# Chunked scan of an RWKV-7 layer: products paired on the array's quadrants, level operands in three buffers

## The reference, cut to what matters

```python
def rwkv_scan(r, decay, k, v, a_vec, b_vec, s0):
    def step(s, inp):
        r_t, w_t, k_t, v_t, a_t, b_t = inp
        sa = jnp.einsum('bhij,bhj->bhi', s, a_t)
        s = s * w_t[:, :, None, :] + sa[..., None] * b_t[:, :, None, :] + v_t[..., None] * k_t[:, :, None, :]
        return s, jnp.einsum('bhij,bhj->bhi', s, r_t)
    s, o = lax.scan(step, s0.astype(jnp.float32), xs)
```

## Time and profile before

| | us |
|---|---|
| three runs | 3109.29, 3109.90, 3113.63 (median 3109.90) |
| profiled execution | 3110.74 |
| its span | 3109.1 |
| mean granted TensorE clock of it | 0.974 |
| TensorE busy | 2955.9 (95%) |
| VectorE, ScalarE, GpSimd busy | 1796.6, 1132.4, 793.0 |
| the scan, first product to end | 1099.9 to 1329.5 |

### The profile page before, as it was taken

One profiled execution on the slowest core, in us unless ns is written; L12 is line 12 of the kernel. 1 busy time (PEld: TensorE's weight loads), 2 busy tenths in 40 slices (PEclk: granted clock), 3 DMA queues, 4 the chain that ended last, 5 costly groups with the idle time before them and its releaser, 6 DMA issues. The chain is left out here.

```text
span 3109.1 us, 65634 instructions
## 1 busy us (share of the span) xinstructions
PE 2955.9 (95%) x27498; PEld 2794.9 (90%) x27498; DVE 1796.6 (58%) x2864; ACT 1132.4 (36%) x2182; POOL 793.0 (26%) x884
## 2 busy tenths in 40 slices
PE   8999999998999989979899989999998999999998
PEld 8999999998999978838777569999998999999998
DVE  7777774565545656566554552343325877775445
ACT  5333334343112233344664351221143433334333
POOL 3555451023001124240003000000015455553003
PEclk9999999998999999979999999999998999999999
DMA  6566568554422120011015641212123466667763
GB/s 174 177 196 202 184 194 246 173 176 135 129 73 65 55 90 4 18 28 48 11 46 171 220 170 51 52 41 65 31 78 100 138 193 194 190 195 228 220 184 111
DMA packets 416735, 393.37 MB, mean 127 GB/s; under 512 B 50584, under 2 KB 367809, under 8 KB 415674
## 3 DMA queue, kind: packets, MB, share of 16 engines
q1 hardware_dynamic: 383418, 277.05, 29.8%
q0 software_dynamic: 31984, 112.13, 11.0%
q10 hardware_dynamic: 1040, 0.00, 0.0%
HBM read 283.59 MB, written 105.53 MB: 125 GB/s over the span
## 5 line engine op out<-in xcount | busy, mean ns | idle before, releaser
L2167 PE MATMUL banks<-hid_pieces,dn_high 128*128 128x258 f32 x2464 | 452.9, 287 | 7.5 <-DVE hid_pieces L2109 7.5
L1911 PE MATMUL banks<-x_pieces,gate_pieces 128*128 128x258 f32 x3360 | 415.2, 283 | 1.0 <-DVE sq L2005 0.9
L1911 PE MATMUL banks<-x_pieces,up_pieces 128*128 128x258 f32 x3360 | 414.4, 283 | 0.0
L1911 PEld LDWEIGHTS banks<-x_pieces,gate_pieces 128*128 128x128 f32 x3360 | 408.9, 189 | 1.7 <-DVE sq L2005 1.4
L1911 PEld LDWEIGHTS banks<-x_pieces,up_pieces 128*128 128x128 f32 x3360 | 408.6, 189 | 0.2 <-ACT sq L1947 0.2
L2167 PEld LDWEIGHTS banks<-hid_pieces,dn_high 128*128 128x128 f32 x2464 | 386.1, 192 | 8.1 <-issue 7.9
L2167 PE MATMUL banks<-hid_pieces,dn_part 128*128 128x258 f32 x1232 | 349.5, 284 | 0.0
L1167 PEld LDWEIGHTS banks<-XG,pR 128*128 128x128 f32 (+1 forms) x1800 | 286.1, 189 | 10.4 <-issue 6.1
L1167 PE MATMUL banks<-XG,pR 128*128 128x344 f32 (+1 forms) x1800 | 291.5, 323 | 3.7 <-DVE pR L2702 2.9
L1167 PE MATMUL banks<-XR,mg_gate 128*128 128x344 f32 x1728 | 283.3, 319 | 1.3 <-PEq L53 1.3
L1167 PEld LDWEIGHTS banks<-XR,mg_gate 128*128 128x128 f32 x1728 | 273.9, 188 | 1.6 <-issue 1.6
(11 more groups left out here) (567 smaller groups left out, 5499.0 us busy)
## 6 DMA issues: line engine op xcount, KB each, us to landing
hid_spill<-h_stage SPq DMA_DIRECT2D x44, 516.0 KB, 4.2
chain_slot<-hid_spill POOLq DMA_DIRECT2D x64, 258.0 KB, 3.8
t_sums<-chain_slot POOLq DMA_DIRECT2D x64, 258.0 KB, 2.7
dn_low<-w_sums SPq DMA_DIRECT2D x32, 384.0 KB, 3.6
praw<-in_w_in SPq DMA_DIRECT2D x24, 512.0 KB, 4.2
sq<-in_w_in SPq DMA_DIRECT2D x24, 512.0 KB, 4.1
chain_slot<-in_ffn_down POOLq DMA_DIRECT2D x46, 256.0 KB, 4.2
w_sums<-chain_slot POOLq DMA_DIRECT2D x46, 256.0 KB, 3.3
```

The source lines that it names most:

```text
L1911: ins = k.nc.tensor.matmul(out, self.w[m][:, a, w, f * P:(f + 1) * P], self.x[p][:, b, x, f * TQ:(f + 1) * TQ], start=first and f == 0 and ...
L2167: ins = k.nc.tensor.matmul(k.ps[2 * j + q][:, 0:TQ], a[s][:, f * P:(f + 1) * P], k.hid_pieces[m % 2][:, q, f, b, :], start=m in self.FRESH ...
```

## The change

It rewrites the scan's order on four engines; the arithmetic stays.

- Outputs move between halves. `inner`, the first half of `outer`, `solved`, the values' part of the carry and the new transposed inverse write to the other half (q' = 1 - q), the second half of `outer` stays on q' = q, and the two are issued alternately, head by head. The outputs of the even chunk alternate with `inner` in level 8, reading the state alternates with the values' part of the odd carry in level 4 and with the odd state's update in level 16.
- The transposed inverse of level 0 is made by TensorE from Tm (`turned_inverse`, 16 products a round) and copied by ScalarE; VectorE's two operations for it go. The transposed sums of both chunks lie in one bank (3) and are added by one operation of 512 columns (`TTs`).
- ScalarE copies G1 and G2 raw; GpSimd masks the parts that outputs and carries read (`G1r`, `G2`). Tm of both chunks is masked and gets its identity in one operation each.
- Level operands lie in a ring of three buffers (`masked`), so a mask waits for the product three before it.
- g1 and g3 of the next round are issued in level 32; the even chunk's carry too. After the loop the last two chunks are finished one after the other.
- `SampleStep` uses two banks instead of three for its transposes.

```diff
-    Tm, NT_, Ym, Wm, Um = (two((4 + 2 * m) * NU) for m in range(5))
+    TTs = [work[:, 2 * z * NU:2 * (z + 1) * NU] for z in R2]
+    Tm, Ym, Wm, Um = (two(m * NU) for m in (4, 8, 10, 12))
+    both_Tm = work[:, 4 * NU:6 * NU].rearrange("p (s h c) -> p s h c", s=2, h=RT)
+    ring = [view(work, m * NU, CH) for m in (6, 7, 15)]
-    Yb, Zb, Wb, Sb, Ob = (0, 1), (2, 3), 5, 6, 7
+    Yb, Zb, TTb, Wb, Sb, Ob, pair, grams = (0, 1), (2, 4), 3, 5, 5, 7, (6, 7), (5, 6)
...
+    def masked(s, i):
+        return ring[(2 * i + s) % 3]
...
+                        n = 2 * (len(LV) * p + i) + s
+                        if n >= 3:
+                            m = (n - 3) // 2
+                            pe_s.wait(pool, ("Y", m // len(LV), (n - 3) % 2, LV[m % len(LV)]))
...
+            def turned_inverse(p):
+                dve_s.wait(pe, ("TmI", p))
+                if p:
+                    dve_s.wait(pe, ("TT", p - 1, LV[-1]))
+                for s in R2:
+                    ins = both(lambda h, q: mm(lane(half(TTb, s * NU, CH), h, 1 - q), lane(Tm[s], h, q),
+                                               k.ident[64 * q:64 * q + 64, 64 * q:64 * q + 64]))
+                pe_s.done(ins, ("TTi", p))
...
-                pe_s.done(both(lambda h, q: mm(lane(half(Yb[s], 0, CH), h, q), lane(NT_[s], h, q), lane(Tm[s], h, q))),
-                          ("Y", p, s, l))
+            def inner(p, s, l, h):
+                for q in R2:
+                    ins = mm(lane(half(Yb[s], 0, CH), h, 1 - q), lane(masked(s, len(LV) * p + LV.index(l)), h, q), lane(Tm[s], h, q))
+                return ins
...
+            def outer_turned(p, s, h):
+                for q in R2:
+                    ins = mm(lane(half(TTb, s * NU, CH), h, q), lane(Ym[s], h, q), lane(TT[p % 2][s], h, q))
+                return ins
+
+            def outer(p, s, h):
+                for q in R2:
+                    ins = mm(lane(half(Zb[s], 0, CH), h, 1 - q), lane(TT[p % 2][s], h, q), lane(Ym[s], h, q))
+                return ins
...
                 for l in LV:
+                    for s in R2:
+                        inner_open(p, s, l)
+                        for h in H4:
+                            ins = inner(p, s, l, h)
+                            if past and l == 8:
+                                last = output(a, 2 * s + h // 2, h % 2)
+                        pe_s.done(ins, ("Y", p, s, l))
...
+                    if l == 32 and more:
+                        gram(p + 1, "g1")
+                        gram(p + 1, "g3")
...
+                    for s in R2:
+                        outer_open(p, s, l)
+                        for h in H4:
+                            ins = outer_turned(p, s, h)
+                            if l < LV[-1]:
+                                ins = outer(p, s, h)
+                        pe_s.done(ins, ("Z", p, s, l))
...
+                    if l == 32:
+                        carry_even(2 * p)
+                        if more:
+                            turned_inverse(p + 1)
...
                     for s in R2:
-                        dve_s.done(nc.vector.tensor_tensor(G1[z][s], half(s, 0, 2 * CH), k.gram_mask, ALU.mult), ("G1", p, s))
...
+                    dve_s.done(nc.vector.tensor_tensor(TTs[z], TTs[z], k.ps[TTb], ALU.add), ("TT", p, l))
```

More of the change, by code:

```diff
@@ new lines, in turned_inverse, with carried_state @@
+            def turned_inverse(p):
+                dve_s.wait(pe, ("TmI", p))
+                if p:
+                    dve_s.wait(pe, ("TT", p - 1, LV[-1]))
[3 more added lines that the diff above has]
+                pe_s.done(ins, ("TTi", p))
+            def carried_state(c, first):
+                kn, out = now(k.A, 0, c), half(Wb, 0, CH)
+                return both(lambda h, q: mm(lane(out, h, 1 - side(c, q)), lane(kn, h, q), lane(ST[c % 3], h, q),
+                                            start=first and h == 0, stop=not first and h == RT - 1))
@@ L440, in carried_state, with carried_value, carry_even @@
+            def carried_value(c, h, first):
+                z, s, out = c // 2 % 2, c % 2, half(Wb, 0, CH)
+                for q in R2:
+                    ins = mm(lane(out, h, 1 - q), lane(G2[z][s], h, q), lane(Vm[z][s], h, q), start=first and h == 0,
+                             stop=not first and h == RT - 1)
+                return ins
+            def carry_even(c):
+                act_s.wait(pe, ("VB", c // 2, 0))
+                pool_s.wait(pe, ("G2", c // 2, 0))
                 if c:
@@ L443, in carried_state @@
                     pe.wait_ge(zeroed.sem, 1)
[L444 to L457, removed]
+                if c + 2 < NCH:
+                    dve_s.wait(pe, ("Tm", c // 2 + 1))
@@ new lines, in carry_odd, with state_and_read @@
+            def carry_odd(b):
+                dve_s.wait(pe, ("state", b - 1))
+                pe_s.wait(pe, ("value", b))
+                pe_s.done(carried_state(b, False), ("W", b))
+            def state_and_read(b):
+                state_open(b)
+                act_s.wait(pe, ("O", b - 1))
+                for i in range(2 * RT):
+                    if i < RT:
+                        ins = read_state(b, i)
+                        if i == RT - 1:
+                            pe_s.done(ins, ("read", b))
+                    last = state(b, i // 2, i % 2)
+                pe_s.done(last, ("S", b))
@@ L582, in _ @@
+            pe_s.wait(pe, ("read", b))
+            output_all(b)
         @block.scalar
@@ L586, in copy, with one, carried, solved @@
                 act_s.done(nc.scalar.activation(out, x, ACT.Copy), done)
+            def one(out, x, step):
+                copy(out, x, step, step)
+            def carried(c):
+                one(Wm[c % 2], half(Wb, 0, CH), ("W", c))
+            def solved(c):
+                one(Um[c % 2], half(Wb, NU, CH), ("U", c))
+            def output(c):
+                one(k.C[:, 0:4, c * CH:(c + 1) * CH], half(Ob, 0, CH), ("O", c))
+            def grams_of(p):
+                for s in R2:
+                    copy(G1[p % 2][s], half(Zb[s], 0, 2 * CH), ("G1", p, s), ("g1", p))
@@ L672 @@
+            for c in (2 * NP - 2, 2 * NP - 1):
+                total(c)
+                state(c)
+                if c % 2 == 0:
+                    query.invert(dve)
+            sample.on_dve(dve, len(sample.order))
 class QuerySquares:
```

460 lines of the change are left out of this document (250 added, 210 removed).

## The result

The changed kernel takes **3122.39 us** (median of 7 runs, 3119.12 to 3128.85), the kernel before 3111.76 beside it (7 runs): a ratio of 1.003, 95% interval 1.0017 to 1.0042. That is 10.6 us slower. The forecast was 3107 us, range 3088 to 3121: wrong in sign, and the time lies outside the range.

A forecast was written before the change was run, and what follows sets the result against it. Fetching TensorE's instructions in packets of 256 was taken to bound the scan. Terms of 24.7 + 166.8 + 25.0 + 9.8 = 226.3 us against 229.6 gave 3.3 us less, 3107 us, range 3088 to 3121.

The forecast's parts named there:

- That fetching bounds the scan: Scan: each packet of 256 TensorE instructions costs its work or about 3.4 to 4 us of fetching, whichever is longer.
- The number of packets: Scan: more products and waits raise TensorE's instruction packets from 7.08 to 7.38 a round.
- The price in a steady round: Rounds 1 to 6: 7.38 packets at 3.77 us, 27.8 us a round, 166.8 us in all.
- The opening and round 0: Scan's start, now with the next round's grams and first carry: 6.56 packets at 3.77 us, 24.7 us.
- round 7: Last full round, making no grams for a next one: 6.63 packets, 25.0 us.
- The other engines at nothing: VectorE, ScalarE and GpSimd in the scan: all under 16 us of a round of 27, so they cost nothing.
- The end: Chunks 14 and 15 finished one after the other: a chain of 9.8 us, where it was 11.8 us.
- A: Rival, scan: every fetch is a short one, 3.45 us a packet; 18 us less, 3089 us; chance 0.13.
- B: Rival, scan: fetching is not the limit; rounds of 21 us, 55 us less, 3055 us; chance 0.09.
- C: Rival, scan: idle TensorE lowers the granted clock in eight of 14 places; 17.6 us more, 3125 us; chance 0.15.
- D: Rival, paired products: pairs sharing rows don't overlap; packets cover it, about 3109 us; chance 0.08.

The follow-up runs named there:

- e1: Changed kernel with 352 of a round's 384 paired records put back on their former two quadrants; ratio 1.0027 to the kernel before, +9.0 us.
- e4: Kernel before with 64 products of each round issued a second time, 256 instructions more a round; +30.5 us, ratio 1.0106.
- e8: Kernel before with 624 already satisfied wait instructions added on TensorE; +15.9 us, ratio 1.0059.
- e9: Changed kernel with 518 TensorE instructions fewer: 24 transposes a round joined two by two, issued in one block, covered waits left out; ratio 1.0001 to the kernel before.
- e11: Changed kernel without pairing and with the transposed inverse made by VectorE, 519 instructions fewer; +2.6 us over the kernel before, ratio 1.0005.
- e2: Changed kernel with the first round's g2 moved back to the scan's start, behind g3; +4.7 us over the kernel before, ratio 1.0013.
- e12: Changed kernel with all savings: unpaired, inverse by VectorE, joined transposes in blocks, covered waits out, first g2 early; ratio 0.9996 to the kernel before.
- e3: Changed kernel with 24 of a round's 48 transposes joined two by two, in one pass, in turn with the others; +11.7 us over the kernel before, ratio 1.0042.
- e6: Changed kernel with 24 transposes a round joined two by two in two passes, in turn with others, covered waits out; +31.1 us over the kernel before, ratio 1.0097.
- e10: Kernel before with joined transposes in blocks and covered waits left out, 454 instructions fewer; +19.4 us, ratio 1.0061.
- e7: Kernel before with 24 transposes a round joined two by two, in turn with others, and covered waits left out; +61.9 us, ratio 1.0198.

## Why the prediction was wrong

- **That fetching bounds the scan: right.** 28 us of TensorE's work left and the scan grew; e1 gave the work back and the total did not move; e4 and e8 added instructions and paid, e9 and e11 took them out and gained; and 47 of TensorE's 50 stops end just after a packet has come. The Trainium skill, page "Runtime: NRT & Kernel Launch", section "Instruction fetch mechanics", has the cost of crossing a block of instructions mostly hidden; in this scan it is not, with 51.9 us of stops behind such transfers.
- **The number of packets: right.** 7.38 a round and two more in all; 59 were counted.
- **The price in a steady round: right.** Rounds 1 to 6 take 168.8 us (1131.50 to 1300.32) for the forecast's 166.8: 44.3 packets at 3.81 us, forecast 3.77.
- **The opening and round 0: the step that failed.** "1,680 / 256 = 6.56 packets x 3.77 = 24.7 us" measured 32.69, 8.0 of the 11.2 us by which the sum fell short (rounds 1 to 6 have 2.0, round 7 1.6, and the end was 0.5 us shorter than forecast). The steady price was taken for packets that never had it: from the first transfer to the sixth, five packets cost 25.2 us after the change and 25.5 before. After the change one of them alone took 8.64 us (the transfers start at 1102.23 and 1110.87), and in it TensorE waited 1.89 us for VectorE to finish Tm and then ran at 1.2 GHz until 1109.61. The text had seen the 27.07 us of the earlier trace rows, put them down to levels that wait for each other, and let them vanish. The mean clock of 0.81 says that some 12 us of the new opening ran at 1.2 GHz, but e2, which raised it to 0.93, won 1.0 us of that stretch: there the slow packet took 6.20 us and a later one 6.50 in place of 4.97. The transfers themselves are no slower in the opening (0.9 to 1.4 us, as later), though the DMA engines move 183 GB/s there and 4 to 5 in the rounds behind. What sets the price of these packets in either kernel stays open.
- **What lies under it:** an ideal price for the new kernel was set against a measured total of the old. The same rule gives the kernel before 57.07 x 3.77 = 215 us, and it took 229.5; it gives the changed kernel 59.41 x 3.77 = 224 us, and it took 237.5. So some 14 us of slow packets (opening, end, and half clock, which the price left out) are in both kernels. Rule against rule, the change is 2.34 packets x 3.77 = 8.8 us slower, 3119 us, which is the result within its noise. The sign was in the text's own counts.
- **The other engines at nothing: right.** TensorE's longest wait for a copy in the scan is 1.3 us, for VectorE's masked Tm with its identity 2.1 us, once, in the opening; and e11 shows no cost of the new masks, order and sums that can be told from noise.
- **The end: right in size,** 9.30 us for 9.8.
- **The rivals.** A: the mean price stayed at 3.8, not 3.45. B: full rounds of 27.3 to 28.8 us, not 21. C came nearest in time (3125) but not in cause: rounds 2 to 7 run at a clock of 1.00, with TensorE idle for 6 to 8 us of each 27 to 29. D: 14.8 ns; the pairs overlap.

## What to carry to other kernels

Where a bound is priced by a rule, apply the rule to the kernel before as well, and forecast the difference of the two sums; what the rule misses of the old total stays in the new one. On an engine that runs thousands of tiny products, count its instructions, waits and weight loads included, before its busy time: here 256 of them cost 3.8 to 4 us whether a round held 21 or 25 us of work. A change that shortens the work and adds instructions then loses. A cut of instructions gains only until the work itself fills the packets (e12); a cut of both was not tried here.

## What the runs showed of the hardware that was not expected

- Where one queue fetches TensorE's instructions in packets of 256, TensorE goes on 1.1 to 1.7 us after a packet has come, and the fetch is not hidden: 47 of its 50 stops in the changed kernel's scan, 51.9 us of 237.5.
- Transposes on a tile of 64x128 among those of 64x64 cost far more than the products they save: 0.20 us to the next record behind one and 0.15 us ahead of one (e3, e6), and 0.11 us from one to the next in a block of them (e9, e10), for 15.0 ns on four quadrants of one shape.
- Two quadrants in the same rows run as fast as two in different rows: the 64x64 transposes of e10's block start two every 59 ns, 29.5 ns each, beside 29.2.
- The granted clock fell again and again in or behind stretches in which TensorE shows as fully busy with few records (e7: 73 in 10.01 us, once a round; e10: 65 in 4.18 us, in four rounds), and not in rounds 2 to 7 of the changed kernel, where it was idle for a quarter of the time between dense bursts. What the single falls of the other runs follow was not worked out.
- A wait that is already satisfied costs TensorE about 25 ns, its share of a packet included (e8: 15.9 us for 624).
